# Nine idle products left out of TensorE's stream in a router and its pass tables (one core)

## The chip, the cores and the metric

The kernel runs on one core of one Trainium2 chip. The metric is the device time of one execution in microseconds. Before the change it is 1088.43 us (median of 3 runs, 1087.82 to 1088.95).

## The reference

One layer over 512 tokens of width 1024, all in float32. Three branches (an RWKV-7 recurrence over 8 heads, a spatial gating unit, a causal convolution of 31 taps) are gated and merged, multiplied with `w_out`, added to the input and normalised. A grouped mixture of experts follows:

```
scores = sigmoid(x @ router_w)                    # 512 x 32
sel    = scores + router_b                        # 4 groups of 8 experts
grp    = argmax over groups of (sum of the two largest sel of the group)
expert = the two largest sel in that group; gate = their scores, normalised
h = silu(x @ w_gate[e]) * (x @ w_up[e]);  y += gate * (h @ w_down[e])
out = layer_norm(2**0.25 * x + y)
```

## The kernel before, in words

Each engine has a program of its own, and they meet at semaphores.

TensorE (PE) first does the input projection, the branches and the merge (to about 583 us of the profiled execution). With the first layer norm, the router runs for two token tiles and then for the other two. VectorE (DVE) does the selection in `best_group` (lines 1155 to 1183) and `pick` (1185 to 1201), a chain of small dependent steps. After each step the helper `then` raises `s_dve` by one and VectorE waits for it; at five places in the second half the count is kept in a list `marks`.

From the choice VectorE and TensorE work out where each token goes. `counted` (L1680 to L1686) sums `chosen` into ranks in PSUM. VectorE compares these with slot numbers (L1241), and 16 matmuls at L1702 gather the rows of the first pass; ScalarE (ACT) copies them out (L806), TensorE transposes them in `turn(0)` (L1714), ScalarE copies again (L808). Meanwhile VectorE goes on to the pass numbers (L1244 to L1277); ScalarE scales eight masks (L812), after L808 in its program. Then 32 matmuls at L1727 (16 pairs) build the pass tables, VectorE reads them (L1293 to L1301), and the experts begin.

In the expert stage each expert is one pass or more of 64 slots: L1744 (gate and up), L1714, L1733, L1754 (transposes and statistics), L1765 (down). There are 33 passes here. The weights of an expert are 6 MB in six chunks of 1 MB, in four sets of buffers. The sync engine (SP) has one queue for all weight loads: the last preloads (L434) wait for `s_onehot` (L1702 done) together with `s_x1st` (rows of x1 stored), then for `s_tab` (tables read); four loads of the last norm's rows follow (L471), and then `reload` (L480), which waits chunk by chunk for TensorE's `s_used`.

The function that the change leaves unused, and the two places that call it:

```
def keep_clock(columns):
    pe.matmul(proj[:, 0, 0:columns], C("ident"), const[:, at:at + columns], start=True, stop=True)
```

Nothing reads what it writes. It is called once at each of the five marks, between the two calls of `counted`, and four times after `turn(0)`, each time with 384 columns. A float32 product is two MATMUL records of the profile.

Of the kernel before, what the change touches and what calls it, by code (L numbers as in the profile page):

```python
# [16 lines left out]
P = 128  # L17
# [139 lines left out]
def program(nc, x_tok, xT, w_in, par, table, lora, rows, sgu_b, sgu_wT, w_o, w_out, router_w, zeros, w_gu, w_down, out):  # L157
    with ExitStack() as ctx:
# [3 lines left out]
        def sem(name):  # L162
            return ctx.enter_context(nc.semaphore(name))
# [21 lines left out]
        def C(name):  # L185
            at, n = CONSTS[name]
            return const[:, at:at + n]
# [156 lines left out]
        s_dve = sem("dve_seq")  # L344
# [45 lines left out]
        marks = []  # L390
# [983 lines left out]
        def _(pe):  # L1374
# [298 lines left out]
            def keep_clock(columns):  # L1673
                at = CONSTS["ones"][0]
                pe.matmul(proj[:, 0, 0:columns], C("ident"), const[:, at:at + columns], start=True, stop=True)

            def counted(lo, first, last):

                if first:
                    pe.matmul(bank[:, 1, 0:(TT + 1) * N_EXP], C("ones"), chosen[:, 0:1, :].broadcast_to([P, TT + 1, N_EXP]),  # L1680
                              start=True, stop=False)
                for c in (lo, lo + 1):
                    at, n = N_EXP * (c + 1), TT - c
                    pe.matmul(bank[:, 1, at:at + N_EXP * n], C("ones"), chosen[:, c + 1:c + 2, :].broadcast_to([P, n, N_EXP]),
                              start=False, stop=False)
                return pe.matmul(bank[:, 1, N_EXP * lo:N_EXP * lo + 2 * N_EXP], C("earlier"), chosen[:, lo + 1:lo + 3, :],  # L1686
                                 start=False, stop=last)

            pe.wait_ge(s_chosen, 1)
            counted(0, True, False)  # L1690
            for mark, n in marks:
                pe.wait_ge(s_dve, mark)
                for _ in range(n):
                    keep_clock(3 * P)
            pe.wait_ge(s_chosen, 2)
            counted(2, False, True).then_inc(s_rank, 1)

# [8 lines left out]
            def turn(p, first=False):  # L1706

                if first:
                    pe.wait_ge(s_copied, 3)
                else:  # L1710
                    pe.wait_ge(s_xe, p * 16)
                    pe.wait_ge(s_xeT, p)
                for c in range(4):
                    ins = pe.transpose(bank[:, 2, c * P:(c + 1) * P], xe[:, c * P:(c + 1) * P], C("ident"))  # L1714
                ins.then_inc(s_xeTp, 1)

            turn(0, first=True)
            for _ in range(4):
                keep_clock(3 * P)

            for n in range(TOPK * TT):
                if n % 2 == 0:
                    pe.wait_ge(s_hot, n // 2 + 2)
# [120 lines left out]
```

## Time and profile before

| | |
|---|---|
| median of 3 runs | 1088.43 us |
| the profiled execution | 1088.21 us, span 1086.4 us |
| granted TensorE clock, mean | 0.997 |
| PE, DVE, ACT, POOL busy | 91%, 43%, 27%, 22% of the span |
| matmuls of the nine products (L1675) | 18 records |

Busy time of an engine is its share of the span from the first to the last instruction. The granted clock is 1.00 where TensorE has its full 2.4 GHz and 0.50 where it has 1.2 GHz. Lines of the profile are lines of the kernel; a line in a helper stands for all calls of the helper.

### The profile page before, as it was taken

What the parts mean: (1) busy time and instruction counts of PE and PEld (TensorE: products, weight loads), DVE (VectorE), ACT (ScalarE), POOL (GpSimd) and SP (SyncE); (2) the same over time, 40 slices, a digit from 0 to 9 for tenths busy, and PEclk for the clock granted to TensorE, in tenths of its full rate; (3) what the DMA queues carried; (4) which work ended last, traced back from release to release, by engine and by line L of the source; (5) the groups of instructions that cost most, each with busy time, mean ns of one, the idle gap of its engine ahead of it and who ended that gap; (6) DMA issues with size and microseconds to landing.
All of it is one profiled execution on the core that took longest, in us unless ns stands there. A gap on an engine that the chain in (4) does not pass through costs nothing.

```text
span 1086.4 us, 16711 instructions
## 1 busy us (share of the span) xinstructions
PE 992.4 (91%) x6132; PEld 457.5 (42%) x6133; DVE 466.0 (43%) x1036; ACT 292.2 (27%) x488; POOL 236.5 (22%) x336
## 2 busy tenths in 40 slices
PE   7999999999999999999998888888888888887774
PEld 3644466457447546644444333333333333322221
DVE  0696453463363454232326433444444443442333
ACT  1113322222232231200014233333333333332321
POOL 2000010010010001013115233333333333332332
PEclk9999999999999999999999999999999999999998
DMA  9432211220221120464746999999999999999992
GB/s 279 125 78 59 77 40 35 64 59 22 59 59 41 39 60 21 156 210 183 285 183 252 344 415 414 403 416 417 415 416 414 416 415 416 414 415 415 417 401 103
DMA packets 96896, 256.62 MB, mean 236 GB/s; under 512 B 17484, under 2 KB 62540, under 8 KB 72016
## 3 DMA queue, kind: packets, MB, share of 16 engines
q1 hardware_dynamic: 85024, 240.57, 58.1%
q0 software_dynamic: 11024, 13.20, 3.6%
q10 hardware_dynamic: 800, 2.15, 0.5%
q8 instruction: 37, 0.61, 0.2%
q14 instruction: 11, 0.09, 0.0%
HBM read 260.66 MB, written 21.23 MB: 259 GB/s over the span
## 4 chain that ended last, share of the span: by engine, by line
PE 52%; DMA 16%; DVE 11%; SPq 9%; issue 7%; POOL 2%; ACT 2%; POOLq 1%; DVEq 0%; PEld 0%; ACTq 0%; PEldq 0%
PE proj L1436 12%; PE proj L1395 11%; SPq L480 9%; DMA y_rows<-const,raw 5%; DMA out<-raw 5%; PE proj L1615 5%; PE bank L1526 5%; PE bank L1604 5%; PE bank L1744 3%; DMA xT_sb<-w_gu 3%; DMA pass_sb<-x_rows,raw 2%; PE proj L1403 2%; PE proj L1414 1%; DVE arena L989 1%; PE bank L1765 1%
## 5 line engine op out<-in xcount | busy, mean ns | idle before, releaser
L1436 PE MATMUL proj<-xT_sb,ring 128*128 128x512 f32 x384 | 182.1, 607 | 0.0
L1744 PE MATMUL bank<-arena 128*64 128x512 f32 x544 | 122.6, 596 | 19.2 <-DMA arena<-w_gu 10.2
L1321 DVE TENSOR_TENSOR raw<-bank,const 128x512 f32<-128x512 f32 x33 | 22.9, 693 | 243.8 <-DMA out<-raw 242.9
L1395 PE MATMUL proj<-xT_sb,ring 128*128 128x512 f32 (+1 forms) x272 | 119.1, 595 | 0.0
L1436 PEld LDWEIGHTS proj<-xT_sb,ring 128*128 128x128 f32 x384 | 68.4, 190 | 68.2 <-issue 64.7
L1744 PEld LDWEIGHTS bank<-arena 128*64 128x64 f32 x544 | 42.6, 137 | 99.1 <-issue 81.8
L1395 PEld LDWEIGHTS proj<-xT_sb,ring 128*128 128x128 f32 (+1 forms) x272 | 50.9, 189 | 64.5 <-issue 64.4
L832 ACT ACTIVATE pass_sb<-bank 128x256 f32<-128x256 f32 x33 | 12.7, 384 | 198.8 <-PE bank L1744 198.8
L518 POOL MEMSET arena<- 64x64 f32 x8 | 1.2, 145 | 291.7 <-DVE arena L1006 257.9
L1744 PE MATMUL bank<-gates,arena 128*64 128x512 f32 x256 | 57.4, 597 | 7.9 <-PE bank L1765 4.0
L1526 PEld LDWEIGHTS bank<-arena 64*64 64x64 f32 x1536 | 52.8, 135 | 18.2 <-ACT arena L727 9.1
L569 POOL DMA_INDIRECT const<-y_rows,raw x33 | 34.6, 1049 | 110.0 <-DMA y_rows<-const,raw 109.2
L1615 PE MATMUL proj<-arena 128*128 128x512 f32 x128 | 57.8, 598 | 0.0
L1526 PE MATMUL bank<-arena 64*64 64x64 f32 (+1 forms) x1536 | 56.5, 228 | 0.0
L1765 PE MATMUL bank<-arena,pass_sb 128*64 128x512 f32 x208 | 48.4, 601 | 8.8 <-DVE pass_sb L1310 8.8
L1604 PE MATMUL bank<-branches,arena 128*128 128x512 f32 x128 | 55.4, 594 | 0.9 <-DVE branches L1083 0.9
L845 ACT ACTIVATE const<-bank,raw 128x512 f32<-128x512 f32 x33 | 22.7, 687 | 106.0 <-PE bank L1765 106.0
L727 ACT ACTIVATE arena<-bank 128x256 f32<-128x256 f32 (+1 forms) x64 | 27.5, 437 | 64.6 <-PE bank L1526 59.6
L589 POOL DMA_INDIRECT out<-raw x33 | 33.5, 1014 | 51.9 <-DVE raw L1341 33.4
L630 ACT ACTIVATE gates<-proj 128x512 f32<-128x512 f32 x24 | 14.3, 596 | 104.7 <-PE proj L1436 104.7
L830 ACT ACT_TABLE_LOAD x32 | 41.1, 1283 | 4.0 <-DVE raw L1301 3.1
L825 ACT ACT_TABLE_LOAD x32 | 41.1, 1283 | 0.6
(305 smaller groups left out, 1368.2 us busy)
## 6 DMA issues: line engine op xcount, KB each, us to landing
arena<-w_gu SPq DMA_DIRECT2D x64, 1024.0 KB, 24.7
gates<-w_gu SPq DMA_DIRECT2D x32, 1024.0 KB, 21.9
arena<-w_down SPq DMA_DIRECT2D x24, 1024.0 KB, 25.3
ring<-w_in SPq DMA_DIRECT2D x42, 512.0 KB, 3.9
gates<-w_down SPq DMA_DIRECT2D x16, 1024.0 KB, 23.9
branches<-w_down SPq DMA_DIRECT2D x16, 1024.0 KB, 27.2
xT_sb<-w_gu SPq DMA_DIRECT2D x16, 1024.0 KB, 26.8
ring<-w_gu SPq DMA_DIRECT2D x16, 1024.0 KB, 25.9
```

The lines of the kernel that those rows point to most:

```text
L480: sp.dma_start(w_chunk[b][c], src.rearrange("a p n -> (a p) n")).then_inc(s_w[b][c], 16)
L569: pool.indirect_dma_start(y_low, None, y_dram, bass.IndirectOffsetOnAxis(ap=up_now[:, 0:1], axis=0), bounds_check=last_half_row, oob_is_er ...
L589: pool.indirect_dma_start(out_dram, bass.IndirectOffsetOnAxis(ap=out_now[:, 0:1], axis=0), x2, None, bounds_check=last_half_row, oob_is_er ...
L825: act.activation(warm[:, table:table + 1], warm[:, 0:1], ACT.Sqrt)
L830: act.activation(warm[:, 1:2], warm[:, 0:1], ACT.Silu)
L1395: ins = pe.matmul(proj[0:w, b, :], ring[:, slot, k, 0:w], xT_sb[:, k, :], start=(k == 0), stop=(k == KT - 1))
L1436: ins = pe.matmul(proj[:, gate_at["bank"], :], ring[:, gate_at["slot"], k, :], xT_sb[:, k, :], start=(k == 0), stop=(k == KT - 1))
L1526: ins = pe.matmul(bank[t, 3 * g + b, j * n:j * n + n], lhsT[t, j, :], rhs[t, j, :], start=True, stop=True)
L1604: ins = pe.matmul(bank[:, 3 * (m % 2) + n, :], wo_sb[:, k0 + k, m * P:(m + 1) * P], src[:, k, :], start=(k == 0), stop=(k == nk - 1))
L1615: ins = pe.matmul(proj[:, n % 2, :], merged[:, c, k, :], wout_sb[:, i, k, :], start=(k == 0), stop=(k == KT - 1))
L1744: ins = pe.matmul(bank[SLOTS * h:SLOTS * h + SLOTS, 0, :], xeT[:, k % 4, SLOTS * (k // 4):SLOTS * (k // 4) + SLOTS], gu[k // 2][:, k % 2, ...
L1765: ins = pe.matmul(bank[SLOTS * h:SLOTS * h + SLOTS, 1, :], hT[:, f % 2, SLOTS * (f // 2):SLOTS * (f // 2) + SLOTS], wd[f // 2][:, f % 2, h ...
```

## The change

The loop over the marks between the two calls of `counted`, and the loop of four after `turn(0)`, are taken out. Everything else stays, the list `marks`, VectorE's counts and the helper included.

```diff
             pe.wait_ge(s_chosen, 1)
             counted(0, True, False)
-            for mark, n in marks:
-                pe.wait_ge(s_dve, mark)
-                for _ in range(n):
-                    keep_clock(3 * P)
             pe.wait_ge(s_chosen, 2)
             counted(2, False, True).then_inc(s_rank, 1)
...
             turn(0, first=True)
-            for _ in range(4):
-                keep_clock(3 * P)
-
             for n in range(TOPK * TT):
```

## Rows read from the trace of the kernel before

**Rows 1.** Slices of the page: TensorE's clock and the DMA engines' share.
```profile
PEclk9999999999999999999999999999999999999998
DMA  9432211220221120464746999999999999999992
```
**Rows 2.** Chain of waits around the tables: start us, us, what.
```profile
595.05 0.63 PE bank L1684 x4
595.68 0.26 PE bank L1686 x2
...
595.97 1.00 DVE pass_sb L1241 x4
...
602.40 0.57 DVE late_sb L1277
...
603.00 1.92 ACT late_sb L812 x8
...
605.05 2.18 PE bank L1727 x32
607.23 1.53 issue
```
**Rows 3.** PE in order of time: start, us, line, count, [idle before, releaser].
```profile
589.15 0.35 PE L1686 MATMUL bank<-raw,const 128*128 128x64 f32 x2
...
593.84 0.91 PE L1675 MATMUL proj<-const 128*128 128x384 f32 x2 [0.44 <-DVE late_sb L1198]
...
596.44 3.65 PE L1702 MATMUL bank<-ring,pass_sb 128*64 128x512 f32 x16 [0.51 <-DVE pass_sb L1241]
600.78 0.66 PE L1714 MATMUL bank<-const,pass_sb 128*128 128x128 f32 x4 [0.69 <-ACT pass_sb L806]
601.27 2.75 PE L1675 MATMUL proj<-const 128*128 128x384 f32 x8
```
**Rows 4.** ACT in order of time, around the first pass's rows.
```profile
600.13 0.60 ACT L806 ACTIVATE pass_sb<-bank 128x512 f32<-128x512 f32 x1 [9.49 <-PE bank L1702]
601.47 0.60 ACT L808 ACTIVATE arena<-bank 128x512 f32<-128x512 f32 x1 [0.75 <-PE bank L1714]
```
**Rows 5.** SP's queue in order of time: start, us to issue, what.
```profile
602.32 0.80 SPq L434 DMA_DIRECT2D ring<-w_gu  x2
607.74 0.33 SPq L434 DMA_DIRECT2D late_sb<-w_down  x1
...
611.51 5.90 SPq L480 DMA_DIRECT2D gates<-w_gu  x4
```
**Rows 6.** One stretch, without engines: us, granted clock, DMA share, GB/s.
```profile
601.50:603.00 1.50, 1.00 0.02 5
```
**Rows 7.** One of nine stretches of the experts, PE PEld DVE ACT POOL first.
```profile
966.00:1016.00 50.00, 39.62 (x186) 12.29 (x184) 16.36 (x42) 14.06 (x24) 16.30 (x25) 1.00 1.02 416
```
**Rows 8.** Stretches at the ends of the span: PE busy, granted clock, DMA.
```profile
5.92:10.59 4.67, 4.67 (x6) 1.00 1.05 360
...
1074.19:1078.98 4.79, 0.28 (x4) 1.00 0.11 44
1078.98:1086.00 7.02, 0.00 (x0) 0.50 0.04 16
```
**Rows 9.** L1403 early and later: ns min/median/max, first and last start.
```profile
L1403 PEld LDWEIGHTS proj<-xT_sb,ring x7: 287/337/337, 5.9 to 10.3; 128*128 128x128 f32 x7
L1403 PE MATMUL proj<-xT_sb,ring x6: 721/1062/1221, 5.9 to 10.3; 128*128 128x512 f32 x6
...
L1403 PE MATMUL proj<-xT_sb,ring x27: 592/593/721, 10.3 to 21.6; 128*128 128x512 f32 x27
L1403 PEld LDWEIGHTS proj<-xT_sb,ring x26: 189/191/316, 10.3 to 21.2; 128*128 128x128 f32 x26
```
**Rows 10.** DVE in order of time: one step in each half of the router.
```profile
583.83 0.23 DVE L1193 TENSOR_REDUCE bank<-late_sb 128x2 f32<-128x64 f32 x1
...
594.25 0.23 DVE L1193 TENSOR_REDUCE bank<-late_sb 128x2 f32<-128x64 f32 x1
```

## The prediction

> **What bounds the kernel now.** The slices of the page come first. TensorE has its full clock in every slice but the last, and from about the 24th slice on the DMA engines are full [rows 1]. The stretches of the expert stage say the same in numbers: nine of 50 us lie between 616 and 1066 us, the first eight with a DMA share of 1.01 or 1.02, as in the one shown, where TensorE is busy for only 39.62 of 50 us [rows 7]. So the expert stage is a stream of weights of some 450 us that nothing on TensorE can shorten, and the end of the kernel is where that stream starts plus its length. What counts before it is how early the stream gets going, and whether the DMA engines stand still. They do once: between 601.5 and 603 us their share is 0.02 [rows 6]. After that the sync engine issues two chunks at 602.32, one more when the tables have been read (607.74), and the first reload at 611.51 [rows 5]. The chain of waits shows what leads to the tables: the counts (L1684, L1686), VectorE from L1241 to L1277, ScalarE's eight masks, the 32 table matmuls, 1.53 us of issue [rows 2].
>
> **The products themselves.** Nine float32 products go, 18 records of L1675. Five stand between the two calls of `counted`: TensorE finishes the first call at 589.50 (589.15 + 0.35), and the last product at 594.75 (593.84 + 0.91). Then it waits 0.30 us for VectorE and starts L1684 at 595.05 [rows 2, 3]. Four stand between `turn(0)` and the tables: they run from 601.27 to 604.02, and TensorE then waits 1.03 us for ScalarE's masks, until 605.05 [rows 2, 3]. Both groups end before the thing that their successor waits for, so taking their time away gives 0 on the path. The waits at the marks go with them; VectorE never waits for TensorE there. The counts on `s_dve` stay. No DMA and no instruction of another engine is moved.
>
> **What the products cover.** Without the five, TensorE does nothing from 589.50 to 595.05, 5.55 us. In the whole trace it never stands still for more than 1.53 us between its first matmul and the last pass; there is one place to compare with, the end. After the last burst of matmuls (1074.19) it ran 0.28 us of work in 4.79 us, and from 1078.98 the granted clock is 0.50, that is 1.2 GHz in place of 2.4 [rows 8]. 5.55 us without any work is longer and emptier than 4.79 us. I take it that the clock falls, at about 589.50 + 4.79 = 594.3. At the start of the kernel TensorE was at the lower level too. The clock column does not show it (its record begins later), but the durations do: the matmuls of L1403 took 1062 ns (median) from 5.92 to 10.6 us and 593 ns after, the weight loads 337 against 191 [rows 9]. It came to full speed after 4.67 us of work without a pause [rows 8]. So dense work goes at half rate for 4.67 us.
>
> **Step 1, the counts.** L1684 and L1686 take 0.89 us from 595.05 [rows 2]. At half clock the cost is between 0 (if the clock holds) and 0.89 more (all doubled). They are short products behind full weight loads, so the nearest row is the weight load, 337/191 = 1.76 [rows 9]: 0.89 x 0.76 = 0.7 more. This is on the path at once: VectorE's L1241 and all that follows it, up to L1277, starts 0.7 us later.
>
> **Step 2, the gather of the first rows.** L1702 started at 596.44 and now starts at 597.15. The six short products and the gap ahead of it I don't count as dense work, so full speed is back at 597.15 + 4.67 = 601.82. Until then half of 4.67 = 2.33 us of its 3.65 us are done; the other 1.32 us end at 603.14. It ended at 600.09 before [rows 3], so it is 3.05 us late. If dense work already counts from 595.05, the clock is back at 599.72 and L1702 ends at 602.08, 2.0 us late; if the clock doesn't come back within it, it ends at 604.45, 4.4 us late.
>
> **Step 3, from there to the masks.** ScalarE's copy L806, the four transposes and the copy L808 ended at 602.07, 1.98 us after L1702 [rows 3, 4]. They now end at 603.14 + 1.98 = 605.12. The masks L812 stand behind L808 in ScalarE's program and were held by VectorE until 603.00 [rows 2]; VectorE would let them go at 603.7. So the 0.93 us in which ScalarE stood ready hide that much, the 0.7 us of step 1 are inside this delay and not added to it, and the masks start at 605.15, 2.15 us late. With the early return of the clock it is 602.08 + 1.98 + 0.03 - 603.00 = 1.1 us. With the late one it is 604.45 + 1.98 + 0.5 (the 0.66 us of transposes by 1.76) + 0.03 - 603.00 = 4.0 us.
>
> **Step 4, the tables and the stream.** L1727, the tables, the load at 607.74 and the first reload at 611.51 shift by the same 2.15 us, if the table matmuls run at full clock. The two chunks issued at 602.32 had waited for the stored rows of x1, whose landing doesn't depend on TensorE; L1702 ended 2.2 us before. With L1702 at 603.14 they are issued some 0.9 us later, which alone would be a smaller shift than that of the tables. In all the stream starts 2.15 us later, and nothing behind it gives that back: the DMA engines have no idle share to give (1.01 to 1.02). The profiled execution of 1088.21 us (span 1086.4, and 1.8 around it) becomes 1090.4. The median of the runs lies 0.2 above it, so the forecast is 1088.43 + 2.15 = 1090.6.
>
> **The second pause.** Without the other four products TensorE has nothing to do from the transposes (end about 604.5) to 607.2, 2.7 us; then 2.18 us of L1727 and 1.53 us of issue. That lies between the pauses up to 1.53 us that cost nothing, and the 4.79 us that did. If the clock falls there, L1727 costs between 0 and 2.18 us more. The first expert's matmuls, at half rate for 4.67 us, cost between 0 and 2.3 us more; part of these is hidden, since the chunks in flight keep the DMA share at 1 while TensorE is a little late. I take 0 for the forecast and keep 4.5 for the range.
>
> The trace has no execution of this kernel with another timing of the clock. The Trainium skill, "TensorE: Matmul & The Clock Gate", section "What's actually happening", says that what watches the activity runs free of the kernel's start. By that rule the fall and the return come at another point in each execution, and the time differs between executions by what separates the early and the late case. Only the ends of this span bear on it, one fall and one return, so the trace neither agrees nor disagrees.
>
> **The rivals.**
> (a) The clock falls twice, as in the second pause. For it: the pause of 2.7 us is nearly twice any that the clock survived, and little work surrounds it. Against it: it is far shorter than 4.79 us, and the tables' matmuls end it. Taking half of each bound, 1.1 + 1.2 = 2.3 us on top of 2.15: 1092.9.
> (b) Nothing changes: the clock stays at 2.4 GHz, since the pauses are short against what it takes, or it falls late and is back at once. For it: there is only one fall in the trace to judge by, and it had a pause at the very end. Against it: that fall needed less than 5.55 us and had work in it. It gives 1088.4.
> (c) Faster. While VectorE walks through its chain, each product reads `const` and writes PSUM, where VectorE's small results lie as well. If the products slow VectorE, their absence gives time back on the path from 589.5 to 595.0 and from 602.4 to 605.0, some 8 us. It decides from the point where the clock's price is under the gain: to make up for 2.15 us VectorE would have to need over 27% less time there. With the clock's price gone too and 30% less time (2.4 us) it gives 1086.0. Against it stands the trace: the same reduction took 0.23 us at 583.83, beside dense matmuls of the merge, and 0.23 us at 594.25, beside a product [rows 10]; the other steps of the two halves agree too.
>
> **How the numbers follow.** The forecast has 0.53, with an own range of +1.1 to +4.0 us, 1089.5 to 1092.4; (a) has 0.26, (b) 0.18, (c) 0.03. What a measurement of this kernel can tell from no change is 0.2%, 2.2 us, so the line lies at 1090.6, in the middle of the forecast's own range. Half of the forecast and all of (a) are slower: 0.27 + 0.26, with a little for late returns, 0.55. The other half of it and (b) are within: 0.42. Faster is 0.03. The range of 8 in 10 reaches from (b)'s 1088.2 to 1093.4, over (a) at half of its bounds; the sum of all upper bounds (4.0 + 4.5) lies outside.
>
> **What would show it.** In the profile of the changed kernel: no records of L1675; a granted clock of 0.50 in a stretch between about 594 and 602 us; L1702 at 5 to 7 us in place of 3.65, and its copy L806 at about 603; the masks L812 about 2 us later, and released by ScalarE's own order and not by VectorE; the DMA engines idle longer ahead of the two chunks of the ring or ahead of the table's load; and every stretch of the expert stage as before, only shifted. A clock of 1.00 throughout refutes the forecast and leaves (b). A second stretch at 0.50 at L1727 or in the first pass is (a). If the masks are late by 2 us and the end is not, the claim that the stream's start sets the end is wrong. VectorE's steps shorter than before would be (c).

## The result, and the profile after

The changed kernel takes 1091.3 us (median of 12 runs, 1090.17 to 1092.18), the kernel before 1088.72 us beside it (12 runs, 1087.82 to 1091.53). The ratio is 1.0017, 95% interval 1.0010 to 1.0024, so it is slower by 1.9 us (1.1 to 2.6); the two medians lie 2.6 us apart, at the upper end. The forecast was +2.15 us. The profiled execution took 1091.83 us, its span is 1089.9 us. Its mean clock of 0.983 is the lowest of the twelve runs (the others have 0.986 to 0.990), so it shows more time at half clock than a usual one.

The slices show the clock below full in two places where it wasn't before [rows 1]:

```profile
PEclk9999999999999999999997999989999999999998
DMA  9432311220221120464746899999999999999992
```

TensorE in order of time, the lines of [rows 3] and of the first pass. L1698 is L1702 of before, L1710 is L1714, L1720 is L1727, L1737 is L1744:

```profile
590.78 0.58 PE L1686 MATMUL bank<-raw,const 128*128 128x64 f32 x2
595.77 1.06 PE L1684 MATMUL bank<-raw,const 128*128 128x64 f32 x4 [4.41 <-DVE raw L1201]
596.65 0.67 PE L1686 MATMUL bank<-raw,const 128*128 128x64 f32 x2
597.82 5.81 PE L1698 MATMUL bank<-ring,pass_sb 128*64 128x512 f32 x16 [0.50 <-DVE pass_sb L1241]
604.32 0.66 PE L1710 MATMUL bank<-const,pass_sb 128*128 128x128 f32 x4 [0.69 <-ACT pass_sb L806]
607.55 2.18 PE L1720 MATMUL bank<-late_sb,const 128*64 128x144 f32 x32 [2.57 <-ACT late_sb L812]
611.26 7.09 PE L1737 MATMUL bank<-gates,arena 128*64 128x512 f32 x32 [1.53 <-issue]
```

The gather of the first rows takes 5.81 us and took 3.65. The stretches give the clock at either side (PE, PEld, DVE, ACT and POOL busy, granted clock, DMA share, GB/s):

```profile
588.00:588.40 0.40, 0.00 (x0) 0.00 (x0) 0.36 (x3) 0.36 (x1) 0.40 (x1) 1.00 0.92 389
588.60:602.10 13.50, 8.59 (x28) 5.34 (x30) 10.48 (x57) 2.72 (x4) 4.68 (x2) 0.50 0.92 354
602.30:609.00 6.70, 3.44 (x36) 2.08 (x33) 3.87 (x15) 3.47 (x11) 0.00 (x0) 1.00 0.64 230
```

From 588.6 to 602.1 us TensorE ran at 1.2 GHz. It fell before the long pause (from 591.36), after the short transposes and router matmuls with their waits of 0.5 to 0.7 us, and the second pause, 2.57 us ahead of the tables, left it at 1.00. ScalarE in order of time, and SP's queue, beside [rows 4, 5]:

```profile
603.67 0.60 ACT L806 ACTIVATE pass_sb<-bank 128x512 f32<-128x512 f32 x1 [12.30 <-PE bank L1698]
605.01 0.60 ACT L808 ACTIVATE arena<-bank 128x512 f32<-128x512 f32 x1 [0.75 <-PE bank L1710]
605.51 1.90 ACT L812 ACTIVATE late_sb<-late_sb,raw 128x48 f32<-128x48 f32 x8
```
```profile
603.73 0.80 SPq L434 DMA_DIRECT2D ring<-w_gu  x2
610.24 0.33 SPq L434 DMA_DIRECT2D late_sb<-w_down  x1
...
614.00 5.90 SPq L480 DMA_DIRECT2D gates<-w_gu  x4
```

The masks L812 have no idle time noted before them: they follow L808 in ScalarE's own order, where before they had waited 0.93 us for VectorE. The first reload is issued at 614.00 in place of 611.51. The DMA engines stand idle for longer than before [rows 6]; this stretch has a share of 0.00, and the 1.5 us ahead of it one of 0.34:

```profile
603.00:604.50 1.50, 1.00 0.00 0
```

**Where the 3.5 us of span between the two profiles lie.** (1) 0.58 us arise far ahead of the change: TensorE starts L1627, the last transposes, at 586.21 and not 585.63, and L1590, at 461.73 before, is already late by the same 0.58. The two executions differ there, not the kernels. L1627 after, then before:

```profile
586.21 0.66 PE L1627 MATMUL bank<-const,ring 128*128 128x128 f32 x4 [0.50 <-DVE ring L1102]
```
```profile
585.63 0.66 PE L1627 MATMUL bank<-const,ring 128*128 128x128 f32 x4 [0.50 <-DVE ring L1102]
```
(2) From L1627 to the first reload are 27.79 us and were 25.88: +1.91, the change. (3) From the first reload to the end are 475.9 us and were 474.9: +1.0. The last sits in one place, the expert with two passes, which holds its buffers twice as long. The DMA share in stretches of 2 us there, after and then before (PE busy, clock, share, GB/s):

```profile
694.00:696.00 2.00, 2.00 (x12) 1.00 0.92 380
696.00:698.00 2.00, 2.00 (x12) 1.00 0.65 232
698.00:700.00 2.00, 2.00 (x12) 1.00 0.92 310
```
```profile
692.00:694.00 2.00, 2.00 (x12) 1.00 1.04 380
694.00:696.00 2.00, 2.00 (x12) 1.00 0.92 368
696.00:698.00 2.00, 1.56 (x8) 1.00 1.00 383
```

In the changed kernel's execution the clock fell again from 663.6 to 667.1 us, in a pass; TensorE came later to the double pass, and the DMA engines ran dry for about 1 us. Counted in bytes from the first reload on, the stream of the changed kernel is some 0.1 us behind that of before until 694 us, and some 1.0 us behind from 706 us to beyond 1050 us. Two more falls, from 718.3 to 725.1 and from 899.2 to 902.6 us, made TensorE late by up to 7.0 us against the profile before (counted from the first pass), but the stream lost nothing by them.

### The profile page after: what moved, and what is told of

It is laid out like the page before. It is cut to its first block, busy times and chain, and to the rows that moved or that the text cites. A ratio compares the mean times of both kernels' runs of the same rounds, so it can differ in the third digit from the quotient of the medians.

```text
span 1089.9 us, 16675 instructions
## 1 busy us (share of the span) xinstructions
PE 995.5 (91%) x6114; PEld 459.4 (42%) x6115; DVE 465.9 (43%) x1036; ACT 291.9 (27%) x488; POOL 236.6 (22%) x336
## 3 DMA queue, kind: packets, MB, share of 16 engines
q10 hardware_dynamic: 800, 2.15, 0.5%
## 4 chain that ended last, share of the span: by engine, by line
PE 57%; DMA 16%; DVE 11%; issue 7%; SPq 4%; POOL 2%; ACT 2%; POOLq 1%; DVEq 0%; ACTq 0%
PE proj L1436 12%; PE proj L1395 11%; DMA out<-raw 7%; DMA y_rows<-const,raw 5%; PE proj L1615 5%; PE bank L1526 5%; PE bank L1604 5%; PE bank L1737 5%; SPq L480 4%; PE bank L1758 3%; DMA xT_sb<-w_gu 3%; PE proj L1403 2%; DMA pass_sb<-x_rows,raw 1%; PE proj L1414 1%; DVE arena L989 1%
## 5 line engine op out<-in xcount | busy, mean ns | idle before, releaser
L1737 PE MATMUL bank<-arena 128*64 128x512 f32 x544 | 121.8, 595 | 15.4 <-PE bank L1758 9.7
L1737 PEld LDWEIGHTS bank<-arena 128*64 128x64 f32 x544 | 43.4, 137 | 93.6 <-issue 84.0
L1737 PE MATMUL bank<-gates,arena 128*64 128x512 f32 x256 | 57.4, 596 | 8.0 <-PE bank L1758 4.0
L569 POOL DMA_INDIRECT const<-y_rows,raw x33 | 34.6, 1050 | 111.4 <-DMA y_rows<-const,raw 110.6
```

The lines of the kernel that those rows point to most:

```text
L569: pool.indirect_dma_start(y_low, None, y_dram, bass.IndirectOffsetOnAxis(ap=up_now[:, 0:1], axis=0), bounds_check=last_half_row, oob_is_er ...
L1737: ins = pe.matmul(bank[SLOTS * h:SLOTS * h + SLOTS, 0, :], xeT[:, k % 4, SLOTS * (k // 4):SLOTS * (k // 4) + SLOTS], gu[k // 2][:, k % 2, ...
```

## The experiments

Each is compared with runs of the kernel before beside it on the same chip, on one of three chips. These are 34, 35 and 27 runs, with medians of 1089.32, 1089.12 and 1089.61 us. Each experiment has 10 to 12 runs and one profile, so what a profile shows is one execution. Delays within a profile are counted from the start of L1627, against 25.88 us from there to the first reload in the profile before.

**marks_out**: the kernel before without the loop over the marks.

```diff
-            for mark, n in marks:
-                pe.wait_ge(s_dve, mark)
-                for _ in range(n):
-                    keep_clock(3 * P)
```

> Only the five products at the marks (and their waits) are left out; the four after the first pass's transposes stay. Theory (the clock falls in or around the 5.5 us pause and L1702 runs at half rate): this part carries nearly all of the change, +2 to +2.6 us over the kernel before, L1702 at 5 to 6 us in the profile, the table matmuls 2 to 2.5 us late. Rival 1 (the second pause matters as much): half of it, +1.3 us. Rival 2 (the stretch falls to half clock anyway, in either kernel): no more than +0.5 us.

Measured: 1090.81 us, ratio 1.0019 (1.0010 to 1.0027). The clock was at 0.50 from 591.5 to 601.7, and L1702 (here L1698) took 5.72 us:

```profile
595.47 1.06 PE L1684 MATMUL bank<-raw,const 128*128 128x64 f32 x4 [5.54 <-DVE raw L1201]
...
597.51 5.72 PE L1698 MATMUL bank<-ring,pass_sb 128*64 128x512 f32 x16 [0.50 <-DVE pass_sb L1241]
```

This part alone costs about what the whole change does, by the theory; in the profile the first reload comes 1.69 us late, against 1.91 in the changed kernel. The clock fell 1.6 us after the last matmul ahead of the pause (which ended at 589.93), not 4.79 us after it. Rival 2 is out (interval from +1.1 us); rival 1's +1.3 us is inside the interval.

**four_out**: the kernel before without the four products ahead of the tables.

```diff
             turn(0, first=True)
-            for _ in range(4):
-                keep_clock(3 * P)
```

> Only the four products ahead of the pass tables are left out; the five at the marks stay. Theory: nothing on the path, the clock mostly survives the 3.6 us pause that the VectorE-bound tables leave, 0 to +0.5 us. Rival (a second fall): the table matmuls and the first expert pass at half rate in some executions, +1.5 to +2.5 us.

Measured: 1091.46 us, ratio 1.0019 (1.0009 to 1.0029). The theory fell here and the rival came true. L1702 ran at full clock, and then:

```profile
595.90 3.65 PE L1702 MATMUL bank<-ring,pass_sb 128*64 128x512 f32 x16 [0.50 <-DVE pass_sb L1241]
600.24 0.66 PE L1714 MATMUL bank<-const,pass_sb 128*128 128x128 f32 x4 [0.69 <-ACT pass_sb L806]
604.51 4.11 PE L1724 MATMUL bank<-late_sb,const 128*64 128x144 f32 x32 [3.61 <-ACT late_sb L812]
608.88 7.74 PE L1741 MATMUL bank<-gates,arena 128*64 128x512 f32 x32 [0.26 <-issue]
```

The table matmuls took 4.11 us and take 2.18 at full clock [rows 2]; the clock was at 0.50 from 603.4 to 610.2. From L1627 to the first reload are 27.89 us, +2.01. Of the 1.93 us that the tables lost, the issue time behind them hid 1.27 for the first pass's start (0.26 in place of 1.53), but nothing for VectorE, which reads the tables when they end, and nothing for the load that waits for it (issued at 609.12, +1.92). The profiled execution (1089.86 us) is the second fastest of twelve; five of them lie between 1089.8 and 1090.4 us and seven between 1091.4 and 1094.7, and what the slower ones paid for no profile shows. Each part alone costs 2.1 us by its ratio, and both together 1.9 (2.3 in waits_only, beside these runs): they don't add up. A possible reason is that an execution pays at one place. The profiles of the changed kernel and of waits_only paid at L1702 and had their clock back in time for the tables. tables_first (below) paid at both, so this isn't a rule.

**waits_only**: no products, the waits at the marks kept.

```diff
             for mark, n in marks:
                 pe.wait_ge(s_dve, mark)
-                for _ in range(n):
-                    keep_clock(3 * P)
...
-            for _ in range(4):
-                keep_clock(3 * P)
```

> All nine products are left out and the five waits of TensorE at the marks stay. Theory (the products' effect is their activity, the waits are free): the same time as the changed kernel, +2.6 us over the kernel before. Rival (TensorE's waits on VectorE's count cost or save something by themselves): it differs from the changed kernel by more than 0.5 us.

Measured: 1091.54 us, ratio 1.0021 (1.0012 to 1.0030), like the changed kernel (1.0017). The clock was at 0.50 from 588.7 to 602.3. So the waits do nothing by themselves that intervals of about 1 us to either side could show; the rival's 0.5 us they can't resolve.

**third_columns**: the same nine products with 128 columns.

```diff
-                    keep_clock(3 * P)
+                    keep_clock(P)
...
-                keep_clock(3 * P)
+                keep_clock(P)
```

> The kernel before with the same nine products and marks, each with 128 columns in place of 384. Nothing is left out of the computation. Theory (it is TensorE's activity that holds the clock, and a third of the columns in three pauses of 0.6 us is far less of it): most of the change's cost, +1.5 to +2.6 us, a stretch at 0.50 in the profile between 588 and 612 us. Rival (any work in the pause is enough, however short): 0 to +0.5 us.

Measured: 1090.96 us, ratio 1.0012 (1.0003 to 1.0021): slower than before, by 0.3 to 2.3 us. The profile has the clock at 0.50 from 594.8 to 601.6, in spite of five products of 0.49 us in the pause, with waits of 0.19 to 0.87 us between them:

```profile
594.16 0.49 PE L1675 MATMUL proj<-const 128*128 128x128 f32 x2 [0.87 <-DVE late_sb L1198]
595.37 1.06 PE L1684 MATMUL bank<-raw,const 128*128 128x64 f32 x4 [0.72 <-DVE raw L1201]
...
597.41 5.70 PE L1702 MATMUL bank<-ring,pass_sb 128*64 128x512 f32 x16 [0.50 <-DVE pass_sb L1241]
```

So it isn't the length of one pause; in this execution the longest was under 1 us, and the clock fell. The rival is unlikely: its 0 to +0.5 us and the interval only touch.

**burst**: the five products in one go behind `counted`, no marks.

```diff
-            for mark, n in marks:
-                pe.wait_ge(s_dve, mark)
-                for _ in range(n):
-                    keep_clock(3 * P)
+            for _ in range(5):
+                keep_clock(3 * P)
```

> The kernel before with the five products of the marks in one burst of some 3.4 us right behind the first call of counted, without the waits at the marks; the four ahead of the tables stay. Nothing is left out of the computation. Theory (activity counts and not its spreading; the pause left is about 2.1 us): 0 to +0.7 us, L1702 mostly at 3.65 us. Rival (a pause of 2 us is enough for the clock to fall in about half of the executions): +1 to +2 us.

Measured: 1089.33 us, ratio 0.9999 (0.9990 to 1.0008), the time of the kernel before. In this execution the clock had fallen at 589.0, ahead of the burst, and was back at 592.4 within it:

```profile
591.25 4.03 PE L1675 MATMUL proj<-const 128*128 128x384 f32 x10
595.90 0.63 PE L1684 MATMUL bank<-raw,const 128*128 128x64 f32 x4 [0.61 <-DVE raw L1201]
...
597.28 3.65 PE L1700 MATMUL bank<-ring,pass_sb 128*64 128x512 f32 x16 [0.50 <-DVE pass_sb L1241]
```

The rival is out (the interval ends at +0.9 us). In this profile the clock came back within the burst and stayed, so the products can bring it back as well as hold it, and the marks aren't needed for either.

**masks_late**: the tables held back from ScalarE, with the clock covered (seven products ahead of the tables). DELAY is 9.

```diff
             act.wait_ge(s_hot, 1)
+            for n in range(DELAY):
+                act.activation(proj[:, 1, PASSES * n:PASSES * n + PASSES], C("ident")[:, 0:PASSES], ACT.Copy)
             for n in range(TOPK * TT):
```

> The kernel before, with nine short ScalarE copies (48 columns, some 0.24 us each) put ahead of the eight masks, so that the tables come some 2.1 us later, and seven idle products in place of four ahead of the tables so that the clock holds. Nothing is left out of the computation. Theory (the weights' stream starts with the tables, and its start sets the end one to one): +2.1 us. Rival 1 (slack between tables and stream, or the stream gives time back): +0 to +1 us. Rival 2 (a late start is amplified at the expert with two passes, where the DMA engines run dry): +3 us or more.

Measured: 1090.19 us, ratio 1.0011 (1.0002 to 1.0020). The copies were shorter than I had assumed: masks at 603.33 in place of 602.12, counted from L1627, so 1.2 us of delay and 1.2 us of time by the ratio. That fits one to one, but the interval (+0.2 to +2.2 us) is wider than the effect; it only puts rival 2 out. So it was repeated larger.

**masks_later**: the same with 32 copies of 16 columns (DELAY is 32) and eleven products.

```diff
+            for n in range(DELAY):
+                act.activation(proj[:, 1, 16 * n:16 * n + 16], C("ident")[:, 0:16], ACT.Copy)
```

> As masks_late with 32 short ScalarE copies (16 columns) in place of nine, which should hold the masks some 4.2 us, and eleven idle products ahead of the tables. Nothing is left out of the computation. Theory (the end follows the first reload one to one): the time rises by the delay of the masks that the profile shows, +4 to +4.5 us, and the span less the time of the first reload's issue stays at 475 to 476.5 us. Rival (part of the delay is given back in the expert stage): +2 to +3 us, and that difference falls to 474 or less.

Measured: 1091.66 us, ratio 1.0020 (1.0011 to 1.0029), +1.2 to +3.2 us. The profile has the masks 3.40 us late, not 4.2:

```profile
602.43 3.46 ACT L813 ACTIVATE proj<-const 128x16 f32<-128x16 f32 x32 [0.92 <-DVE late_sb L1280]
605.83 1.90 ACT L815 ACTIVATE late_sb<-late_sb,raw 128x48 f32<-128x48 f32 x8
```
```profile
614.37 1.42 SPq L481 DMA_DIRECT2D gates<-w_gu  x2
```

From L1627 (L1630 here, at 585.08) to the first reload are 29.29 us, +3.41, and from there to the end 475.2, nothing given back. In the runs the time rose by 2.05 between the medians, less than 3.4 and on the rival's side. The two readings don't agree by themselves. Part of the reason may be that the runs of the kernel before carry a cost of their own (next section), which eleven products spare this one; that wasn't tried apart. Runs of like clock lie closer to the profile: those with a mean clock of at least 0.996 have medians of 1091.6 (5 runs of this kernel) and 1088.8 us (8 of the kernel before), +2.8. The rest stays open.

**first_pass_late**: five products between the tables and the first pass, made from `ident`.

```diff
+            for _ in range(5):
+                pe.matmul(proj[:, 0, 0:3 * P].rearrange("p (k t) -> p k t", k=3), C("ident"),
+                          C("ident").unsqueeze(1).broadcast_to([P, 3, P]), start=True, stop=True)
             pe.wait_ge(s_first, 1)
```

> The kernel before with five idle products (3.4 us at full clock) between the table matmuls and the first pass, in place of 1.53 us of issue: the tables and all that SP loads up to the reloads are as early as before, TensorE's passes begin some 2 us later. Nothing is left out of the computation. Theory 1 (what matters is when the reloads get going, and they follow TensorE's first pass with little in reserve): +1 to +2 us. Theory 2 (the DMA engines have enough in flight at that point, only the tables' time counts): 0 to +0.3 us.

Measured: 1090.91 us, ratio 1.0018 (1.0009 to 1.0027). Theory 2 is out. The profile shows two costs, one of them unforeseen:

```profile
591.18 5.65 PE L1675 MATMUL proj<-const 128*128 128x384 f32 x10
596.67 0.53 PE L1684 MATMUL bank<-raw,const 128*128 128x64 f32 x4
...
608.67 3.49 PE L1772 MATMUL proj<-const 128*128 128x384 f32 x10
612.10 7.09 PE L1744 MATMUL bank<-gates,arena 128*64 128x512 f32 x32
```
```profile
602.85 0.81 SPq L434 DMA_DIRECT2D ring<-w_gu  x2
609.25 0.33 SPq L434 DMA_DIRECT2D late_sb<-w_down  x1
...
614.23 6.51 SPq L480 DMA_DIRECT2D gates<-w_gu  x4
```

The clock had fallen at 588.8 here too, and the five marked products themselves ran late: they ended past VectorE, L1684 started without a wait, 10.33 us after L1627 in place of 9.42. So idle products can stand on the path. The load that waits for the tables came 0.8 us late for it; the first reload 2.01 us late, the remaining 1.2 us from the late pass. The first pass began 2.63 us late, the reload came 2.01 us late, so some 0.6 us were in reserve. In the profile before, the reload is set by SP's own queue, 3.77 us after the load that waits for the tables (3.76 in the changed kernel); here it comes 4.98 us after.

**tables_first**: the changed kernel, the masks ahead of L806 and L808, the tables ahead of `turn(0)`. The masks' old place behind L808 is empty, and the counts of `s_copied` that are waited for are exchanged (not shown).

```diff
+            act.wait_ge(s_hot, 1)
+            for n in range(TOPK * TT):
+                ins = act.activation(pass_hot[:, n, 2, :], pass_mask[:, n, :], ACT.Copy, scale=gates_of[:, n:n + 1])
+            ins.then_inc(s_copied, 1)
             act.wait_ge(s_onehot, 1)
...
-            turn(0, first=True)
             for n in range(TOPK * TT):
...
             ins.then_inc(s_tabp, 1)
+            turn(0, first=True)
```

> The changed kernel (no idle products) with the order turned: ScalarE does the eight masks ahead of the copies of the first pass's rows, TensorE does the table matmuls ahead of turn(0). Nothing is left out of the computation. Theory (the slow L1702 reaches the tables only because the masks stand behind the copy L808 in ScalarE's program): the tables come back to VectorE's pace, so of the changed kernel's +2.6 us some 1 to 1.8 us is recovered, +0.8 to +1.6 us over the kernel before. Rival (what is lost is lost at the table matmuls and the first pass at half rate, not at the masks): no recovery, +2.5 us or more.

Measured: 1090.42 us, ratio 1.0015 (1.0004 to 1.0026). The medians lie 1.3 us apart, half of the changed kernel's 2.6, but by the ratio it is 1.6 us and 1.9, and the interval (+0.4 to +2.8 us) doesn't part it from none. The profile shows no gain at all:

```profile
596.26 5.19 PE L1698 MATMUL bank<-ring,pass_sb 128*64 128x512 f32 x16 [0.50 <-DVE pass_sb L1241]
604.87 2.86 PE L1719 MATMUL bank<-late_sb,const 128*64 128x144 f32 x32 [3.42 <-ACT late_sb L807]
...
609.55 8.80 PE L1738 MATMUL bank<-gates,arena 128*64 128x512 f32 x32 [0.77 <-ACT arena L812]
```
```profile
608.24 0.33 SPq L434 DMA_DIRECT2D late_sb<-w_down  x1
...
613.40 6.51 SPq L480 DMA_DIRECT2D gates<-w_gu  x4
```

The masks no longer wait for the slow gather: they start at 602.82, at VectorE's pace, 0.65 us late (counted from L1627, at 584.80 here), and the theory's link is there. But the pause ahead of the tables became 3.42 us, the clock was back at 599.4, fell again at 606.2, and the first pass took 8.80 us and not 7.09. So the load behind the tables is issued 1.33 us late, less than the changed kernel's 1.92, and the first reload 2.72 us late, more than its 1.91. Three of the twelve runs took over 1093 us. Whether the order of the masks is worth anything in the end is not shown.

**filled** and **filled_experts**: the kernel before with more products in the short waits, from the last transposes to the first pass, and in the second also in each pass. The helper `keep_clock` is defined further up for it (not shown).

```diff
+            keep_clock(2 * P)
             turn_half(2 * TT - 1)
+            keep_clock(2 * P)
             router_half(2 * TT - 1)
+            keep_clock(P)
             routed_sums(1)
...
-            for _ in range(4):
+            for _ in range(5):
                 keep_clock(3 * P)
...
             ins.then_inc(s_tabp, 1)
+            for _ in range(2):
+                pe.matmul(proj[:, 0, 0:3 * P].rearrange("p (k t) -> p k t", k=3), C("ident"),
+                          C("ident").unsqueeze(1).broadcast_to([P, 3, P]), start=True, stop=True)
```

> The kernel before with more idle products, all put where TensorE waits: 2, 2 and 1 blocks of 128 columns ahead of the last transposes, the last router matmuls and the last router sums, five in place of four products ahead of the tables, two behind them. Nothing is left out of the computation. Theory (the kernel before also loses its clock in the router stretch in those of its executions in which the granted clock is under 0.995, and these are the slow ones): median 0.5 to 1.2 us below the kernel before, and no clock of 0.50 between 580 and 612 us in the profile. Rival (the pauses under 0.7 us do no harm, the spread has another source): the same time as before, same spread.

Measured: 1089.36 us, ratio 1.0003 (0.9994 to 1.0011); the clock at full from 580 to 612 us. The runs spread less, 1088.34 to 1090.4 against 1087.48 to 1091.15, though they are 11 against 35, and the median didn't fall: of the theory's gain of 0.5 to 1.2 us the interval leaves at most 0.7.

In `filled_experts` this stands twice in each pass as well, ahead of the wait for `s_hT` and behind the last down matmul:

```diff
+                pe.matmul(bank[:, 0, 0:P], C("ident"), C("ident"), start=True, stop=True)
```

> As filled, and in each expert pass two more products of 128 columns, in the two waits of 0.5 to 0.8 us ahead of the down matmuls and of the next pass. Nothing is left out of the computation. Theory: what is lost at half clock in the passes matters only up to the expert with two passes (the DMA engines run dry there), so 0 to 1 us below filled, with a mean clock of 0.998. Rival (TensorE's passes have slack throughout, the DMA engines set the time): the same as filled; or slower by the added work, 33 x 0.1 to 0.2 us, if the waits don't hide it.

Measured: 1089.28 us, ratio 0.9999 (0.9990 to 1.0007); no fall of the clock in the whole span but the last. No gain over filled either (1089.36), as far as 1 us can be told. None of the versions beats the kernel before.

## Why the prediction was right, and where it wasn't

**The products cost nothing on the path**: true in the profile of before, and without them nothing came earlier in the profile after; not true in an execution whose clock has fallen ahead of them (first_pass_late, +0.9 us).

**The clock falls without the five**: the cost is right, the cause is only half right. In all five profiles without the five full products (the changed kernel, marks_out, waits_only, third_columns, tables_first) L1702 met a clock of 0.50 and took 5.19 to 5.81 us; in the eight with them it took 3.65. But the pause didn't make the clock fall as the prediction has it, at 589.50 + 4.79 = 594.3. In the changed kernel it fell at 588.5, 2.3 us after the start of L1627, and the first of the five products comes 4.2 us after it in the profile before. So this fall was no effect of the change. In waits_only, marks_out, tables_first and third_columns it fell at 588.7, 591.5, 589.1 and 594.8. Three kernels that keep the five (masks_late, burst, first_pass_late) show falls at 588.8 to 589.1 as well, after the short router matmuls. The comparison with the end of the kernel (a pause of 4.79 us) was too simple: in six of thirteen profiles the clock fell by 589.1 with no pause of more than 0.7 us in the router stretch ahead, and in the others it held through these matmuls (filled and filled_experts have products between them).

What the five products buy is therefore two things, in about equal parts of these profiles: no later fall (the kernel before, four_out, masks_later), or an early return (592.4, 592.5 and 595.6 us, against 599.4 to 602.3 without them). The return was predicted for 601.8 and came at 602.2. That is partly luck: full speed was counted 4.67 us from the start of the slow L1702, and in the five profiles it came 3.1 to 4.4 us after that start.

The Trainium skill, "TensorE: Matmul & The Clock Gate", section "What's actually happening", says that what watches the activity runs free of the kernel's start. These traces agree: apart from filled and filled_experts TensorE has the same instructions up to about 589 us, and the clock fell at 588.5, at 589.1, later or not at all.

**Step 1**, 0.7 us for the counts: L1684 to the end of L1686 was 0.89 us and is 1.55, +0.66. **Step 2**, L1702 3.05 us late: counted from the start of L1684 it ends 7.86 us after (603.63) and ended 5.04 after, +2.82. **Step 3**, masks 2.15 us late: 9.74 us after L1684 against 7.95, +1.79. The missing 0.36 is 0.2 from step 2, 0.1 from ScalarE starting L812 before L808 had quite ended, and rounding. **Step 4**: the two chunks of the ring +0.83 for a forecast of some 0.9, and from L1627 to the reload +1.91 for a forecast of +2.15. Of the 1.91, 0.14 arise ahead of L1684, where L1645, whose sums VectorE reads, took 1.02 us at 1.2 GHz and 0.63 before; the prediction had nothing there.

Over the profiles of all thirteen kernels the first reload was issued from 611.07 to 614.37 us, and from it to the end it was always 474.9 to 476.5 us. In the profiles the claim that the stream's start sets the end holds; the run times of masks_later rose by less than its delay, which stays open. "Nothing behind it gives that back" holds in the profiles too (TensorE is busier there than the one stretch of [rows 7] says: 42.9 to 44.8 of 50 us in the seven ahead of it), but something behind takes: when the clock falls at about 663 us (the changed kernel, third_columns, first_pass_late) that difference is 475.9, 476.0 and 476.5; with a fall at 647.1 us (burst, masks_late) it is 475.2 and 475.7, and without a fall in the passes ahead of the double one 474.9 to 475.6. This wasn't in the sum, and the sign "every stretch of the expert stage as before, only shifted" did not come. Nothing shows that these falls follow from the change: burst and masks_late keep the five products and have one too. In the profiled execution the two errors, 0.24 us too much ahead of the stream and 1.0 us left out behind it, have opposite signs.

**The second pause** was mis-sized. I took 0 and kept 4.5 for the range. By itself it costs 1 to 3 us (four_out), as much as the first. The forecast held because the two don't add up, not because this term was small; the prediction gave no such reason, so here it was lucky.

**The base.** The profile of before had no fall of the clock until its last microseconds. Of its 96 runs beside the experiments, the 32 with a mean clock over 0.9955 have a median of 1088.56 us, the 47 at or below 0.9945 one of 1090.08. So the clock and the time go together there (correlation -0.55; -0.47 to -0.63 on each chip). The kernel before may pay in part of its executions what the changed one, with a mean clock of at most 0.990 in all twelve runs, pays in all. That this is the same fall, in the router, isn't shown: filled has none there in its profile, and its median stayed.

Rival (a), a second fall at the tables or in the first pass, was not what the profile had, and its +4.5 us lie outside the interval. Rival (b) is out by the interval. Rival (c) is out: VectorE's L1193 takes 0.23 us at 594.98 in the changed kernel, with TensorE idle, as it did before [rows 10]:

```profile
594.98 0.23 DVE L1193 TENSOR_REDUCE bank<-late_sb 128x2 f32<-128x64 f32 x1
```

## What to carry to other kernels

Between short dependent steps, read the granted clock around the stretch, in several executions: products that nobody reads can be worth 2 us where a path runs through matmuls behind them, and one execution may not show it. Take the price from the work that comes next on the path at half rate, less what the waits beside it hide, and follow it to the transfer that it releases; if that starts a saturated stream, the delay went to the end whole in these profiles. Don't price two such gaps as a sum without a test: here each alone cost about as much as both.

## What wasn't expected of the hardware

The clock fell with TensorE partly busy and no pause over 0.9 us in it (third_columns, at 594.8), and fell inside expert passes (663.6 to 667.1, 718.3 to 725.1 and 899.2 to 902.6 in the changed kernel's profile), where the same instructions held it in the profile before. The counts (short matmuls behind full weight loads) at 1.2 GHz took 1.55/0.89 = 1.7 times as long, the table matmuls 4.11/2.18 = 1.9 times. Back-to-back ScalarE copies of 16 columns follow each other every 0.11 us (3.46/32).
